# Attention norm's factor moved from x to the rotary tables, V and gates, and the last expert pair's rows sent by halves

## The reference, cut to what matters

```
for l in range(DEPTH):                       # DEPTH = 2
    h = rms_norm(x, attn_norm_g[l])          # x * rsqrt(mean(x*x) + eps) * g
    proj = einsum('bsd,de->bse', h, w_in[l]) # q, k, v of four attentions, two gates
    q, k = apply_rope(q, cos, sin), apply_rope(k, cos, sin)
    ya = banded_attention(...) @ w_branch_a[l]        # with sinks
    yb = mixture of three dilated_attention(...) @ w_branch_b[l]
    x = x + (sigmoid(gate_a) * ya + sigmoid(gate_b) * yb) @ w_out[l]
    x = x + hier_moe(rms_norm(x, ffn_norm_g[l]))      # top-1 group, top-2 of its 8 experts
return rms_norm(x, final_norm_g)
```

## Time and profile before

| | us |
|---|---|
| median of 3 runs (1303.5 to 1305.22) | 1304.12 |
| time of the profiled execution | 1303.61 |
| its span (first to last instruction) | 1301.8 |
| PE busy, share of the span | 1196.3 (92%) |
| DVE, ACT, POOL busy | 567.2, 408.6, 239.8 |
| mean granted PE clock, share of full | 0.976 |

### The profile page before, as it was taken

The page is one execution under the profiler, slowest core; times in us unless marked ns, Lnnn a source line. Parts: engine busy times, 40 slices in busy tenths (PEclk is TensorE's granted clock), DMA queues, the critical chain, the costliest instruction groups (busy, mean ns, idle before and its releaser), DMA issues.

```text
span 1301.8 us, 17478 instructions
## 1 busy us (share of the span) xinstructions
PE 1196.3 (92%) x6408; PEld 794.4 (61%) x6408; DVE 567.2 (44%) x1392; ACT 408.6 (31%) x822; POOL 239.8 (18%) x177
## 2 busy tenths in 40 slices
PE   7999998999999999889599999989999999988971
PEld 5777787888886343223177777778888853433320
DVE  4667865323345232112456677553234452222115
ACT  5444456333242110001244444562333411100002
POOL 0405320222200111111012254102221001111100
PEclk9999999999999999889899999999999999999996
DMA  5423321653666999999833333126437689999995
GB/s 201 118 81 98 98 82 35 210 192 97 240 229 245 404 424 422 423 422 411 315 98 88 89 113 98 43 93 217 160 99 279 217 301 422 424 422 427 417 412 221
DMA packets 69152, 305.51 MB, mean 235 GB/s; under 512 B 11798, under 2 KB 12054, under 8 KB 58832
## 3 DMA queue, kind: packets, MB, share of 16 engines
q1 hardware_dynamic: 58624, 282.45, 57.7%
q0 software_dynamic: 10304, 21.23, 4.5%
q10 hardware_dynamic: 144, 0.77, 0.2%
HBM read 288.63 MB, written 23.07 MB: 239 GB/s over the span
## 4 chain that ended last, share of the span: by engine, by line
PE 69%; DMA 12%; SPq 8%; ACT 4%; DVE 4%; issue 2%; DVEq 1%; POOLq 0%; ACTq 0%
PE bank L535 14%; PE bank L537 14%; PE bank L536 14%; PE bank L845 10%; DMA gu<-in_gu_w 9%; PE bank L861 5%; SPq L396 4%; SPq L401 3%; PE bank L644 2%; PE bank L673 2%; PE bank L608 1%; DMA raw<-in_stream 1%; PE bank L815 1%; PE bank L840 1%; PE bank L777 1%
## 5 line engine op out<-in xcount | busy, mean ns | idle before, releaser
L845 PE MATMUL bank<-gu,xgt 128*64 128x512 f32 x1024 | 239.7, 618 | 37.6 <-DMA gu<-in_gu_w 36.4
L535 PE MATMUL bank<-h_hi,w_hi 128*128 128x512 f32 x640 | 253.6, 396 | 4.4 <-DVE h_lo L1293 3.4
L537 PE MATMUL bank<-h_hi,w_lo 128*128 128x512 f32 x640 | 249.5, 390 | 0.0
L536 PE MATMUL bank<-h_lo,w_hi 128*128 128x512 f32 x640 | 249.2, 389 | 0.0
L1248 DVE TENSOR_TENSOR w_lo<-raw,w_hi 128x1024 fp32r<-128x1024 f32 x100 | 131.0, 1311 | 165.2 <-ACT w_hi L973 165.2
L845 PEld LDWEIGHTS bank<-gu,xgt 128*64 128x64 f32 x1024 | 75.0, 142 | 196.5 <-issue 149.6
L535 PEld LDWEIGHTS bank<-h_hi,w_hi 128*128 128x128 f32 x640 | 120.2, 188 | 30.3 <-DVE w_lo L1248 3.6
L537 PEld LDWEIGHTS bank<-h_hi,w_lo 128*128 128x128 f32 x640 | 120.1, 188 | 25.4
L536 PEld LDWEIGHTS bank<-h_lo,w_hi 128*128 128x128 f32 x640 | 120.3, 188 | 23.6
L973 ACT ACTIVATE w_hi<-raw 128x1024 fp32r<-128x1024 f32 x100 | 105.3, 1053 | 58.4 <-PE bank L537 54.9
L861 PE MATMUL bank<-dn,zt 128*64 128x512 f32 x512 | 116.9, 599 | 6.0 <-ACT zt L1209 2.8
(11 more groups left out here) (189 smaller groups left out, 1613.3 us busy)
## 6 DMA issues: line engine op xcount, KB each, us to landing
gu<-in_gu_w SPq DMA_DIRECT2D x18, 4096.0 KB, 31.1
raw<-in_stream SPq DMA_DIRECT2D x112, 512.0 KB, 3.6
dn<-in_dn_w SPq DMA_DIRECT2D x18, 2048.0 KB, 31.8
gu<-in_gu_w SPq DMA_DIRECT2D x32, 1024.0 KB, 13.9
dn<-in_dn_w SPq DMA_DIRECT2D x20, 1024.0 KB, 19.0
gu<-in_gu_w SPq DMA_DIRECT2D x32, 512.0 KB, 5.3
swp<-pj SPq DMA_DIRECT2D x136, 64.0 KB, 2.5
dn<-in_dn_w SPq DMA_DIRECT2D x16, 512.0 KB, 4.8
```

The lines of the kernel that those rows point to most:

```text
L535: mm(dst, ah, bh, start=start, stop=False)
L536: mm(dst, ah, bl, start=False, stop=False)
L537: return mm(dst, al, bh, start=False, stop=stop)
L845: last = mm(bank[b][e * CAP:(e + 1) * CAP, :], xgt[:, x_s, k, e * CAP:(e + 1) * CAP], gu[w_s][:, e, k, :], start=k == 0, stop=k == KD - 1)
```

## The change

**First edit: the norm's factor.** `scale_x`, `xn` and their semaphores go. PE transposes x itself as soon as a tile is there; `h_hi` and `h_lo` are made from it per block k (`xt_ok` counts blocks of the last tile). The factor is needed only later: the squares of tiles 0 to 2 stay in front, the fourth, one root and one `rstd` over four tiles come behind `h_hi` and `h_lo`. A new step `("norm", 0)` stands in `ORDER` behind tile 1: PE spreads the four factors of each partition over a row of 512 (`factors`, four matmuls against the identity), DVE copies that to `r_row` and makes `cos_r` = cos times r; POOL multiplies the first V by r and makes `sin_r`. The rotary tiles use `cos_r` and `sin_r`. Each of the seven V tiles gets a POOL multiplication by r before its turn (`vr_ok`), and `("turn", 0)` moves behind tile 2. Each gate gets a DVE multiplication from its bank to `sg` before ACT's sigmoid (`gm_ok`).

With it the beginning is reordered: the constants come in two parts (480 columns with the identity first, 1024 of the tables later, issued by ACT behind `split_hi` of tile 1), and SP's order becomes x0, weight tile 0, x1, x2, parameters, x3, weight tile 1. The filler matmuls on PE become 384, 2x256 and 3x128 columns between the four tiles' transposes. Tile 1's split comes behind `h_hi` and `h_lo` in the first layer.

**Second edit: the last pair.** `down_pair` of pair 15 finishes the left 512 columns first and counts `dn_ok` twice (hence `DOWNS = PAIRS + 1`). POOL scatters the left half of the rows when ACT has copied it, and the right half when DVE has. SP loads the second rows in two sets of four loads of 128x512, each behind its scatter, and DVE adds them in eight steps, all left ones first. The parameters of the next layer are loaded ahead of them. Slot numbers of the last pair are also stored doubled, for rows of half length.

```diff
         if i == 1:
+            order.append(("norm", 0))
+        if i == 2:
             order.append(("turn", 0))
...
+                    if i == 0 and l == 0:
+                        load_x(0)
+                    if i == 1 and l == 0:
+                        load_x(1)
+                        load_x(2)
+                        sp.dma_start(par[:, :], params[0, :, :]).then_inc(par_ld, 16)
+                        load_x(3)
                     if i >= 2 or l == 0:
                         load_tile(l, i)
...
-                load_rows(1)
+                need(sp, ysc[0], (l + 1) * (PAIRS // 2) * 16)
+                sp.wait_ge(left_ok, (l + 1) * 16)
+                load_rows(1, slice(0, T), yl_ld[1])
+                need(sp, ysc[1], (l + 1) * (PAIRS // 2) * 16)
+                load_rows(1, slice(T, D), x_ld)
...
-                for n in range(TT - 2):
-                    pe.wait_ge(x_ok, l * TT + n + 1)
-                    keep_busy(bank[7][:, :], 2)
-                for t in (0, 1, 3, 2):
-                    pe.wait_ge(xn_ok[t], l + 1)
-                    for k in range(KD):
-                        last = nc.tensor.transpose(bank[k][:, t * P:(t + 1) * P], xn[:, t, k * P:(k + 1) * P], ident)
-                    last.then_inc(xt_ok, 1)
+                for t in range(TT):
+                    pe.wait_ge(x_ok, l * TT + t + 1)
+                    for k in K_ORDER:
+                        last = nc.tensor.transpose(bank[k][:, t * P:(t + 1) * P], x[:, t, k * P:(k + 1) * P], ident)
+                        if t == TT - 1:
+                            last.then_inc(xt_ok, 1)
+                    if t < TT - 1:
+                        keep_busy(bank[7][:, (t + 1) * P:min(t + 4, TT) * P], t + 1)
...
+                def factors(_i, l=l):
+                    pe.wait_ge(rs_ok, l + 1)
+                    for t in range(TT):
+                        last = mm(bank[3][:, t * P:(t + 1) * P], rs[:, t:t + 1].to_broadcast([P, P]), ident, start=True, stop=True)
+                    last.then_inc(rr_ok, 1)
...
             def transpose_v ...
-                    pe.wait_ge(pj_act, l * NQ + i + 1)
+                    pe.wait_ge(vr_ok, l * VS[NQ] + n + 1)
...
+                    if n == PAIRS - 1:
+                        for f in range(2):
+                            pe.wait_ge(dn_part[n][f], (l + 1) * 16)
+                        for half in range(2):
+                            for f in range(2):
+                                last = down_step(n % RING, half, f)
+                            last.then_inc(dn_ok, 1)
...
             # ACT
-            act.dma_start(cst[:, :], consts).then_inc(cst_ld, 16)
+            act.dma_start(cst[:, C_ID:C_END], consts[:, C_ID:C_END]).then_inc(cst_ld, 16)
...
+                for n, k in enumerate(K_ORDER):
+                    act.wait_ge(xt_ok, l * KD + n + 1)
+                    run(h_hi[:, k, :], bank[k][:, :], ACT.Identity, scale=g_col[:, k:k + 1]).then_inc(hhi_ok, 1)
                 if l == 0:
                     split_hi(l, 1)
+                    act.dma_start(cst[:, 0:C_ID], consts[:, 0:C_ID]).then_inc(cst_ld, 16)
+                square(3, l)
+                root(slice(0, 4), 2 * l * TT + 3, eps)
...
                     for gte in range(2):
-                        act.wait_ge(w_used, l * NT + it * 6 + i0 + gte + 1)
-                        run(sg[:, half, gte, :], bank[4 * half + gte][:, :], ACT.Sigmoid).then_inc(sig_ok, 1)
+                        act.wait_ge(gm_ok, l * 2 * KD + it * 4 + 2 * half + gte + 1)
+                        run(sg[:, half, gte, :], sg[:, half, gte, :], ACT.Sigmoid).then_inc(sig_ok, 1)
...
             # DVE
+                def factors(l=l):
+                    dve.wait_ge(rr_ok, l + 1)
+                    v.tensor_copy(r_row[:, :], bank[3][:, :]).then_inc(rc_ok, 1)
+                    dve.wait_ge(cst_ld, 32)
+                    v.drain()
+                    tt(cos_r[:, :], c(C_COS, T), r_row[:, :], ALU.mult)
+                    v.drain()
...
+                    for gte in range(2):
+                        dve.wait_ge(w_used, l * NT + it * 6 + i0 + gte + 1)
+                        tt(sg[:, half, gte, :], bank[4 * half + gte][:, :], r_row[:, :], ALU.mult).then_inc(gm_ok, 1)
                     split_lo(l, i0 + 3, it)
...
-                for t in range(TT):
-                    dve.wait_ge(yl_ld[1][t], (l + 1) * 16)
-                    stt(x[:, t, :], yld[:, 1, t, :], w_second[:, t:t + 1], x[:, t, :], ALU.mult, ALU.add).then_inc(x_ok, 1)
-                pair(0, n).then_inc(rs_ok, 2)
+                for half, done, times in ((slice(0, T), yl_ld[1], l + 1), (slice(T, D), x_ld, l + 2)):
+                    for t in range(TT):
+                        dve.wait_ge(done[t], times * 16)
+                        last = stt(x[:, t, half], yld[:, 1, t, half], w_second[:, t:t + 1], x[:, t, half], ALU.mult, ALU.add)
+                        if done is x_ld:
+                            last.then_inc(x_ok, 1)
...
             # POOL, V tiles
+                        pool.wait_ge(pj_act, l * NQ + i + 1)
+                        pool.wait_ge(rc_ok, l + 1)
+                            g.tensor_tensor(vt[:, n % 2, :], vt[:, n % 2, :], r_row[:, :], ALU.mult).then_inc(vr_ok, 1)
+                            pool.wait_ge(cst_ld, 32)
+                            g.tensor_tensor(sin_r[:, :], c(C_SIN, T), r_row[:, :], ALU.mult).then_inc(sn_ok, 1)
...
             # POOL, last pair
+                pool.wait_ge(ya_ok, n0 + PAIRS)
+                scatter_half(0, left_ok)
+                pool.wait_ge(yd_ok, n0 + PAIRS)
+                scatter_half(1, ysc[1])
```

More of the change, by code:

```diff
@@ L181, in hybrid_encoder @@
     pt = [at(f"pt{i}", a, [2, MB], FP32) for i, a in enumerate((R_Q + 42 * KB, R_W + 40 * KB))]
+    cos_r = at("cos_r", R_W + 44 * KB, [T], FP32)
+    sin_r = at("sin_r", R_W + 46 * KB, [T], FP32)
     m_hi = at("m_hi", R_Q, [TT, KD, P], F32R)
@@ L272, in hybrid_encoder @@
         cst_ld, par_ld, gr_ld = sems("cst_ld", "par_ld", "gr_ld")
-        x_ld = sems(*(f"x_ld{t}" for t in range(TT)))
         raw_ld = sems("raw_ld0", "raw_ld1")
@@ L1218, in _ @@
                     split_hi(l + 1, 0)
+                    act.wait_ge(dn_ok, (l + 1) * DOWNS)
                     split_hi(l + 1, 1)
                 load_table()
-                norm(l + 1)
+                if l + 1 < L:
+                    for t in range(TT - 1):
+                        square(t, l + 1)
+                else:
+                    norm(L)
         @block.vector
@@ L1294, in _ @@
                         ALU.subtract).then_inc(hlo_ok, 1)
+                if l == 0:
+                    split_lo(l, 1)
+                rstd(slice(0, 4), 2 * l * TT + 3, eps.to_broadcast([P, 4])).then_inc(rs_ok, 1)
                 if l == 0:
@@ L1556, in slots @@
                         half = slice(e * CAP, (e + 1) * CAP)
+                        if n == PAIRS - 1:
+                            ts(slot[half, 0, :], bank[7][half, 2 * e:2 * e + 2], float(2 * T), 2.0, ALU.add, ALU.mult)
                         last = ts(slot[half, n, :], bank[7][half, 2 * e:2 * e + 2], float(2 * T), None, ALU.add)
@@ L1777, in _ @@
                         scatter(n - 4, ysc[n % 2])
-                for n in range(PAIRS - 4, PAIRS):
+                for n in range(PAIRS - 4, PAIRS - 1):
                     pool.wait_ge(ya_ok, n0 + n + 1)
```

104 lines of the change are left out of this document (53 added, 51 removed).

## The result

The changed kernel took 1309.79 us (median of 20 runs), the kernel before 1304.42 us (20 runs beside it): ratio 1.0037, 95% interval 1.0026 to 1.0047, so some 4.8 us **slower**. I had said 1301.2, with 1297.0 to 1306.3 as the range. The profiled execution has a span of 1309.2, against 1301.8; that is 7.4, or 2.6 more than the medians say.

What follows compares the result with a forecast made beforehand. PE was taken to bound the gate and branch stage, DMA (98%) the experts, leaving only seams to shorten. Gains 5.5 less losses 2.65 gave net 2.85: profiled time 1300.75, median 1301.2, range 1297.0 to 1306.3.

Steps and rivals of the forecast that it cites:

- the one on the last pair: Last pair's down matmuls: left half 1.8 earlier, right half unchanged; halves worth 0.8 at the layer seam.
- Start, 2.4 forecast: Kernel start: first projection matmul at 16.1 instead of 18.50, a gain of 2.4 (1.8 to 3.6).
- Loss 0.25: First layer, between tiles 0 and 1: tile 1's split comes behind h_lo, costing 0.25 (0 to 0.6).
- Seam, 2.2 forecast: Between the layers: next h_hi at 655.2 instead of 657.37, a gain of 2.2 (1.2 to 3.4).
- Factor row, 0.5 per layer: Between tiles 1 and 2: four 128-column matmuls in PE's queue cost 0.5 per layer (0.45 to 0.8).
- Contention behind tile 1, 0.3 per layer: Behind tile 1: DVE and POOL slow each other, delaying split_lo(3), a loss of 0.3 per layer (0 to 1.1).
- Gates, 0.8: Sixteen gate halves: added DVE product cuts cover to 0.17, losing 0.05 per half, 0.8 in all (0 to 3).
- Clock: PE's turns before the projection: they hold the clock and were assumed also to raise it from 0.50.
- rival B: The clock doesn't rise on turns, each layer's first projection tile starts at the lower level: +4.6, 1305.8; chance 0.2.
- End, 0.9: Kernel end: final(0) starts at 1291.5 instead of 1292.46, a gain of 0.9 (0 to 1.6).
- rival D: Gates: product, hand-overs and sigmoid delay split_lo, so PE stalls at each of sixteen halves, 7.7 in all: 1308; chance 0.07.
- signs of being wrong: x loads much later than 14, PE waiting for w_lo at each half, or a layer's first tile at half clock.

Runs made afterwards that it cites:

- 3: Changed kernel with the last pair's down matmuls by weight part first, so the wait on the second part goes: 1.0031 of the kernel before (changed kernel 1.0037).
- 4: Kernel before with only the last pair's down matmuls half by half after both weight parts, whole rows and one signal: 1.0030 of the kernel before.
- 5: Kernel before with rows sent, loaded and added by halves, down matmuls by weight part first: 1.0030 of the kernel before.
- 6: Norm edit alone, factor by turns, x loaded early, with second adds left halves first, rows sent whole: 1.0018 of the kernel before, against 0.9963.
- 9: Norm edit alone, factor by turns, with x1 ahead of the weight tile, which no longer waits for constants: 0.9963 of the kernel before, against 0.9977.
- 8: Factor row by four turns instead of products: changed kernel 1.0027 against 1.0037, norm edit alone 0.9977 against 0.9985, ratios to the kernel before.
- 11: Norm edit alone, factor by turns, x early, without POOL's V products (output differs): 0.9937 of the kernel before, against 0.9963.
- 10: Filler cut: norm edit, factor by turns, x early (0.9963) with less 0.9949, none 0.9917; changed kernel without 1.0003; kernel before without its own 1.0021.

## Why the prediction was wrong, point by point

- **The step that failed** is the one on the last pair: "The last pair's down matmuls now finish the left half 1.8 earlier", with a right half "where it did", and from it 0.8 at the seam and 0.9 at the end. Shown: in half-major order PE waits 1.9 and 1.6 for the second weight part; the left half is 0.3 earlier at the seam and 0.2 later at the end, the right half 1.4 later (3 and 4 above), up to 3.1 with the clock; and DVE, which I had free at 644.9, is 1.7 later, since its copy of the right half stands ahead of its first adds. And all left halves before all right ones make every tile whole late: 3.3 and 1.1 us with the old norm (5), 5.9 and 2.7 by the order of adds alone (6). I wrote "x0 done 648.3" and "x0 is whole only at 1287.3" and used them in the chains, yet compared only the last add with before, instead of the first whole tile (10.45 behind yb before, 13.78 behind it in the changed kernel, at 651.13). Halves by themselves: +6.5, where I had a gain of 1.7.
- **Start, 2.4 forecast.** 0.6 in the profile, and 0.8 to 1.0 in three others with the same start; the norm edit alone had 2.9 (13.97), with the turns of tile 1 already at the upper level (9). So the gain hangs on when the clock rises. The direction was right, three inputs were off: constants at 5.4 (I took 4.5), x1 at 10.5 (9.4), and filler "2.1 us at the lower level" that took 4.2 (1.49 + 1.92 + 0.83, the last at the upper level), since each product is two records. Tile 1's split, "Loss 0.25", cost 0.13 (the first matmul of tile 1 comes 0.36 behind the last of tile 0 instead of 0.23). Without the filler and with x1 earlier, h_hi is at 11.33.
- **Seam, 2.2 forecast.** The norm edit alone makes 3.9 there (21.49 to 17.57), more than I gave the whole; the halves took it away.
- **Factor row, 0.5 per layer.** 0.81, so mis-sized by the same two records; made by turns it is 0.35 (8). The first scores come 1.2 later behind h_hi (46.99 - 16.29 against 46.38 - 16.88).
- **Contention behind tile 1, 0.3 per layer.** It is there: the rope product beside GpSimd's V product took 1.63 instead of 0.69, the split of tile 3 2.31 instead of 1.22. The Trainium skill (GPSIMD Engine Reference, Specifications) lists GpSimd's SBUF interfaces as shared with VectorE, with contention for VectorE instructions that have two SBUF inputs. Both of these have two, and their times agree. PE's waits for w_lo in attention rose from 0.3 to 1.3 in the first layer and from 0.6 to 0.8 in the second, 1.2 together where I had 0.6: inside the bounds, but the longest new one (0.43 at 55.88) stands far behind tile 3, and no run shows which of them the contention makes. Whether "nothing" holds for the other V products stays open (11).
- **Gates, 0.8.** 0: PE was busy for all 140 us. The split ended at 267.78 and nothing waited for it; from the attention's mix to the first router matmul (374.74 before, 376.57 after) it took 152.64 before and 152.51 after. The split had 0.31 left to the next gate's first matmul at 268.09, so the small cover was read rightly and was enough.
- **Clock.** That turns raise it was an assumption no row had shown; it came out right (10), and rival B with it wrong. What I had not priced is that a stretch with a new wait in it can be followed by the lower clock.
- **End, 0.9.** 0.7 was won behind yb (15.05 to 14.32), and 2.8 lost ahead of it.
- **Rivals.** The outcome is close to rival D's 1308 by number, but its mechanism (gates) did nothing, and none of my rivals was the one that decided. Nor did the signs of being wrong that I had named show it: PE did not wait for w_lo at the halves, and the first tile of a layer ran at the full clock.

Norm edit alone, filler out, factor by turns, x loaded early: **1293.48 us against 1304.94, ratio 0.9917**. The norm edit was worth having; the halves were not, nor was filler between the turns.

## What to carry to other kernels

When a result is sent in smaller pieces, look at when the first consumer's unit is whole, not when the last piece arrives: here the consumer works by row tiles, so pieces by columns finish every tile late. Before reordering matmuls for an earlier first half, list which weights the new order needs first. Filler for the clock paid here only in time that was idle anyway; move the work in front of it and the filler has to be weighed again.

## What the runs showed of the hardware

- Turns by TensorE both hold the clock and raise it: from 0.50 to 1.00 (0.99) with no other PE work, in two kernels (10). The Trainium skill (TensorE: Matmul & The Clock Gate, PE-mode transpose) says that the full clock doesn't engage for them; these runs disagree.
- A 128-column f32 product with the identity is two records and cost about 0.2 us at the upper level (1.05 for four, 0.81 to the next matmul); a turn of the same block is one record and 0.114 (in the factor row 0.35 for four to the next matmul).
- A wait of 1.6 to 1.9 us ahead of a PE step was followed by a lower clock within it in 6 of 10 cases, adding 1.4 to 1.7 us to a step of 3.65; in the changed kernel PE had worked 0.44 us of the 3.2 and 3.0 before these steps. Behind a wait of 0.47 it never was. What decides between the two outcomes no run here shows.
